# Top-1-group, top-2-expert MoE on one core: experts in fours with 32 places each, rows gathered and results added by one-hot products

## The chip, the cores and the metric

The kernel runs on one core of one Trainium2 chip. The metric is the device time of one execution in microseconds (us). Before the change three runs took 1572.35, 1572.91 and 1574.51 us, with a median of 1572.91 us.

## What is computed

The reference is a two-layer decoder trunk on 512 tokens of width 1024, in float32. Layer 0 mixes tokens with an S5 state space and an RG-LRU, layer 1 with multi-head latent attention. After each mixer comes a mixture of experts (MoE), and this is what the change touches. There are 64 experts in 8 groups of 8. Each token takes its best group and the best two experts in it:

```python
g_sel = jnp.argmax(g_logits, axis=-1)
top_vals, top_idx = lax.top_k(e_in_group, 2)
gates = p_g[:, None] * jax.nn.softmax(top_vals, axis=-1)
expert_id = g_sel[:, None] * 8 + top_idx
def expert_block(xb, e):                 # xb: the rows of the tokens that chose e
    return (silu(xb @ w1[e]) * (xb @ w3[e])) @ w2[e]   # 1024 -> 256 -> 1024
out = zeros.at[token].add(gate * expert_block(...))
```

So 1024 (token, expert) assignments fall on 64 experts, 16 on average, and every expert's three matrices (1 MiB each, 192 MiB for a layer) are read once. Counted from the reference on its own drawn inputs, the assignments of one expert are unequal: in layer 0 five experts have more than 32 (33, 33, 36, 40 and 61), in layer 1 four (33, 34, 37 and 39), and none has more than 64.

## The kernel before

The MoE of a layer is a sweep over 32 pairs of experts. An expert has 64 places (`CAP = 64`), so that a pair fills 128 rows: expert g of the pair sits in columns 64g to 64g+63 of the systolic array. Six experts' weights are in SBUF at a time: `w13[b]` holds w1 and w3 of slot b, `w2[b]` its w2. The slots lie in `ring`, `wbuf` and `region_a`, and belong to pairs in turn.

For a pair, TensorE does in this order: `te_up` (8 blocks of the 1024 inputs times 2 experts, 512 columns each, L1534), `te_xtrans` (8 transposes of the next pair's 128 rows, L1524), `te_hidden` (2 transposes, L1543) and `te_down` (8 products of 512 columns, L1554). A float32 product is carried out as two MATMUL instructions, so `te_up` is 32 of them and `te_down` 16; a transpose is one. ScalarE does the SiLU and half of the evacuations, VectorE the gating product (L1671) and the other half.

The rows come and go through DRAM. The normed rows are stored in `hrow`; GpSimd gathers each expert's rows with an indirect DMA into `xin` (L1478) and scatters its results with another into `ytok` (L1490), in quarters of 16 rows. When all is scattered, SyncE loads `ytok` back (`combine_sync`, L1902), and VectorE adds each token's two rows, weighted, to `x` (`gathered`, L558). The first pair's rows and the last pair's results go by one-hot products instead (L1280, L1593).

SyncE's queue carries the weight loads, in the order of the pairs: `up_weights_load` (L1744) waits until the slot's last user has done `te_up`, `down_weights_load` (L1749) until it has done `te_down`. The engines run the sweep in hardware loops (`Fori`).

Experts with more assignments than places get overflow blocks: `extra_blocks` runs once before the last pair, on two overflow blocks at a time, `OVPAIR` turns of a loop in which only the first `nov` do anything. With 64 places `nov` is 0 and the whole loop is jumped over.

Of the kernel before, what the change touches and what calls it, by code (L numbers as in the profile page):

```python
# [6 lines left out]
F32 = mybir.dt.float32  # L7
I32 = mybir.dt.int32
# [23 lines left out]
CAP = 64  # L32
QUART = CAP // 4
OVMAX = 2 * T // CAP - 1
NBLK = NE + OVMAX + 1
PAIR = 2 * CAP
NPAIR = NE // 2
# [7 lines left out]
NOROW = 8 * T  # L45
# [3 lines left out]
C_T, C_E, C_I, C_DESC, C_INVF = 576, 1088, 1152, 1168, 1176  # L49
C_ID8 = 1208  # L50
C_END = 1216


def shape_constants():

    c = np.zeros((P, C_END), np.float32)
    r = np.arange(P)
    c[:, C_ID:C_ID + P] = np.eye(P)
    c[:, C_UP:C_UP + P] = r[:, None] < r[None, :]
    c[:, C_ONE:C_ONE + P] = 1.0  # L60
# [8 lines left out]
    c[:, C_ID8:C_ID8 + 8] = r[:, None] + P * np.arange(8)[None, :] - NOROW  # L69
    return c  # L70


def hybrid_decoder(nc, a, out):
    ctx = ExitStack()
    with ctx:
# [25 lines left out]
        id2 = con[:, C_ID2:C_ID2 + CAP]  # L101
# [35 lines left out]
        s_zf = sem("s_zf")  # L137
# [19 lines left out]
        def alink(ins):  # L157
# [7 lines left out]
        junk = [r3[:, 0:1024], extra[:, 2048:3072], extra[:, 0:1024], extra[:, 2560:3584]]  # L165
# [306 lines left out]
        def even_scalar():  # L472
# [28 lines left out]
            S.wait_ge(s_zf, 128)  # L501
# [298 lines left out]
        win = [r2[:, n * KC * HW:(n + 1) * KC * HW].rearrange("p (k n) -> p k n", k=KC) for n in range(2)]  # L800
# [251 lines left out]
        def odd_vector():  # L1052
# [76 lines left out]
            for n in range(H * TC + 7):  # L1129
# [31 lines left out]
        R = extra[:, 2048:3072]  # L1161
        R2 = extra[:, 3072:4096]
# [8 lines left out]
        o2 = R[:, 928:960].rearrange("p (c g) -> p c g", c=TC)  # L1171
        ovb, ovs = R2[:, 64:128], R2[:, 128:192]
        quart, short, wrap, turn16 = R2[:, 0:64], R2[:, 64:128], R2[:, 128:192], R2[:, 448:512]
        place = R2[:, 192:448].rearrange("p (c e) -> p c e", c=TC)
        o12 = R[:, 896:960].rearrange("p (j c e) -> p j c e", j=2, c=TC)
        mm = R2[:, 512:768].rearrange("p (c e) -> p c e", c=TC)
        wk = R2[:, 768:1024].rearrange("p (c e) -> p c e", c=TC)
        gmx, v1, v2, pg, g12, tm = small(4), small(4), small(4), small(4), small(8), small(4)
        destf, blkf, base8, ov8, tm12 = small(8), small(8), small(8), small(8), small(8)
        tmg, gb, vd = small(4), small(4), small(4)  # L1180
        lastf = small(8)
        rk01 = R[:, 960:968].rearrange("p (c g) -> p c g", c=TC)
        ovf = small(17)
        ovw = R[0:1, :].rearrange("p (i e) -> p i e", i=16)
        w13 = [ring[b][:, 0:2, :] for b in range(RING)]
        w13 += [v.rearrange("p (a n) -> p a n", a=2) for v in (wbuf[:, 0:4096], rega[:, :])]
        w2 = [ring[b][:, 2, :] for b in range(RING)] + [wbuf[:, 4096:6144], wbuf[:, 6144:8192]]
        SLOTS = len(w2) // 2
        TURNS = [len(range(b, NPAIR, SLOTS)) for b in range(SLOTS)]


        xin = [regb[:, i * 1024:(i + 1) * 1024] for i in range(2)]
        xtr = [regb[:, 2048 + i * 1024:2048 + (i + 1) * 1024].rearrange("p (k s) -> p k s", k=KC) for i in range(2)]
        hid = [extra[:, i * DE:(i + 1) * DE] for i in range(2)]
        hidT = [extra[:, 512 + i * FC * PAIR:512 + (i + 1) * FC * PAIR].rearrange("p (f s) -> p f s", f=FC)
                for i in range(2)]
        yo = [extra[:, 1024 + i * D:1024 + (i + 1) * D] for i in range(2)]
        hot_s = extra[:, 0:8 * CAP].rearrange("p (j s) -> p j s", j=8)
        hot_b = extra[:, 512:512 + 8 * NE].rearrange("p (j b) -> p j b", j=8)
        oh0 = R[:, 160:672].rearrange("p (c s) -> p c s", c=TC)  # L1200
        hotv_s = R2[:, 192:704].rearrange("p (j s) -> p j s", j=8)
        hotv_b = R2[:, 704:832].rearrange("p (j b) -> p j b", j=8)
        gath = [v.rearrange("p (b d) -> p b d", b=4) for v in (rega[:, :], r0[:, 0:4096])]
        pickT = R2[:, 0:512].rearrange("p (c s) -> p c s", c=TC)
        pick = R2[:, 512:1024].rearrange("p (c s) -> p c s", c=TC)
# [7 lines left out]
        s_oh0 = sem("s_oh0")  # L1213
        s_fr, s_fre = sem("s_fr"), sem("s_fre")
        s_hot, s_hp = sem("s_hot"), sem("s_hp")
        s_dst = sem("s_dst")
        s_ov = sem("s_ov")
        s_hst = sem("s_hst")
        s_pk, s_pkt, s_pke = sem("s_pk"), sem("s_pkt"), sem("s_pke")
        s_fin = sem("s_fin")  # L1220

        ml = {n: [sem(f"{n}{l}") for l in range(2)] for n in (
            "s_xtp", "s_xte", "s_up", "s_si", "s_ac", "s_ht", "s_hte", "s_dn", "s_ye",
            "s_ga", "s_ow", "s_ox", "s_ostep", "s_oys")}
        s_xi = [[sem(f"s_xi{l}{j}") for j in range(2)] for l in range(2)]
        s_yst = [[sem(f"s_yst{l}{j}") for j in range(2)] for l in range(2)]
        s_w13 = [sem(f"s_w13{b}") for b in range(SLOTS)]
        s_w2 = [sem(f"s_w2{b}") for b in range(SLOTS)]  # L1230

# [40 lines left out]

        def first_rows_tensor(l):

            keep_clock(1)

            for c in range(TC):
                TE.wait_ge(s_oh0, TC * l + c + 1)
                for nh in range(2):
                    last = TE.matmul(ps[:, 2 + nh, :], oh0[:, c, :], h[:, c, nh * 512:(nh + 1) * 512],  # L1280
                                     start=c == 0, stop=c == TC - 1)
            last.then_inc(s_fr, 1)

        def first_trans_tensor(l):

            TE.wait_ge(s_fre, 2 * l + 2)
            for k in range(KC):
                last = TE.transpose(ps[:, k // 4, (k % 4) * PAIR:(k % 4 + 1) * PAIR], xin_block(0, k), ident)
            last.then_inc(ml["s_xtp"][l], 1)

        def table_tensor(l):

            for j in range(8):
                TE.wait_ge(s_hot, 9 * l + j + 1)
                last = TE.matmul(ps[0:CAP, 6, 0:NE], hot_s[:, j, :], hot_b[:, j, :], start=j == 0, stop=j == 7)
            last.then_inc(s_hp, 1)

        def extra_table_tensor(l):

            TE.wait_ge(s_hot, 9 * l + 9)  # L1300
            for j in range(8):
                last = TE.matmul(ps[0:CAP, 5, 0:NBLK - NE], hotv_s[:, j, :], hotv_b[:, j, :], start=j == 0, stop=j == 7)
            last.then_inc(s_hp, 1)

        def first_max(oneh, val, best, order):
# [4 lines left out]
            vlink(V.reduce_max(order, t8, AX.X))  # L1310
            tt(oneh, t8, order[:, :, None].to_broadcast([P, TC, 8]), ALU.is_equal)
# [9 lines left out]
        def turned_ranks(rk):  # L1321

            ts(short, quart, CAP / QUART - 1.5, ALU.is_lt)
            stt(turn16.rearrange("p (a e) -> p a e", e=16), quart.rearrange("p (a e) -> p a e", e=16), 1.0,
                con[:, C_I:C_I + 16][:, None, :].to_broadcast([P, NE // 16, 16]), ALU.add, ALU.mult)
            tt(turn16, turn16, short, ALU.mult)
            vlink(V.memset(turn16[:, 0:2], 0.0))
            ts(wrap, quart, float(QUART), ALU.mult, float(QUART + 8 * T), ALU.add)
            stt(wrap, short, -8.0 * T, wrap, ALU.mult, ALU.add)
            wrapb = wrap[:, None, :].to_broadcast([P, TC, NE])  # L1330
            tt(place, rk, turn16[:, None, :].to_broadcast([P, TC, NE]), ALU.add)
            tt(wk, place, wrapb, ALU.is_ge)
            tt(wk, wk, wrapb, ALU.mult)
            tt(place, place, wk, ALU.subtract)

        def route_vector(l):
# [3 lines left out]
            first_max(oh, gl, gmx, tmg)  # L1340
# [31 lines left out]
            for j in range(2, CAP // QUART):  # L1372
                stt(quart, cnt, float(QUART * j), quart, ALU.is_gt, ALU.add)
# [759 lines left out]
```

## Time and profile before

| | |
|---|---|
| median of three runs | 1572.91 us |
| span of the profiled execution, first to last instruction | 1571.5 us |
| TensorE busy | 1344.6 us, 86% of the span |
| VectorE, ScalarE, GpSimd busy | 491.8, 295.4 and 290.5 us |
| MoE sweep of layer 0 on TensorE, first `te_up` to last `te_down` | 246.9 to 747.5 us |
| MoE sweep of layer 1 | 1051.0 to 1554.9 us |

The profiled execution's own time is its span of 1571.5 us, 1.4 us below the median of the runs. PE is TensorE's matmul side and PEld its loads of the stationary operand. Busy shares are averages over stages with different limits, so stages are read one by one.

### The profile page before, as it was taken

What the parts mean: (1) busy time and instruction counts of PE and PEld (TensorE: products, weight loads), DVE (VectorE), ACT (ScalarE), POOL (GpSimd) and SP (SyncE); (2) the same over time, 40 slices, a digit from 0 to 9 for tenths busy, and PEclk for the clock granted to TensorE, in tenths of its full rate; (3) what the DMA queues carried; (4) which work ended last, traced back from release to release, by engine and by line L of the source; (5) the groups of instructions that cost most, each with busy time, mean ns of one, the idle gap of its engine ahead of it and who ended that gap; (6) DMA issues with size and microseconds to landing.
All of it is one profiled execution on the core that took longest, in us unless ns stands there. A gap on an engine that the chain in (4) does not pass through costs nothing.

```text
span 1571.5 us, 19548 instructions
## 1 busy us (share of the span) xinstructions
PE 1344.6 (86%) x6176; PEld 624.6 (40%) x6176; DVE 491.8 (31%) x1034; ACT 295.4 (19%) x584; POOL 290.5 (18%) x412
## 2 busy tenths in 40 slices
PE   7999998987887878878799899999978878878786
PEld 5555463332332323333464565453323323333332
DVE  7996145211111111112605572253111111111114
ACT  6236111110010010101235642111100100101000
POOL 2104002332222222222000000003322222222220
PEclk9999999999899998999799899999999998999999
DMA  5423845999999999999410307049999999999996
GB/s 211 166 103 131 347 176 220 374 393 405 405 397 404 403 396 412 397 401 380 174 54 1 121 1 294 23 172 389 402 394 404 390 392 403 404 411 404 394 397 276
DMA packets 83427, 472.17 MB, mean 300 GB/s; under 512 B 13953, under 2 KB 16145, under 8 KB 32816
## 3 DMA queue, kind: packets, MB, share of 16 engines
q1 hardware_dynamic: 69792, 445.25, 71.7%
q0 software_dynamic: 11568, 19.90, 3.8%
q10 hardware_dynamic: 2016, 6.34, 1.0%
q8 instruction: 33, 0.54, 0.1%
q14 instruction: 18, 0.15, 0.0%
HBM read 453.54 MB, written 27.39 MB: 306 GB/s over the span
## 4 chain that ended last, share of the span: by engine, by line
PE 42%; SPq 35%; DVE 11%; DMA 6%; issue 5%; ACT 1%; DVEq 0%; POOL 0%; ACTq 0%; POOLq 0%
SPq L1744 23%; PE ps L1534 13%; SPq L1749 12%; PE ps L1554 5%; DMA ring<-in_moe_w 4%; PE ps L442 4%; PE ps L885 3%; PE ps L904 2%; PE ps L315 2%; PE ps L908 2%; PE ps L431 2%; PE ps L391 2%; PE ps L1524 1%; DVE extra L549 1%; DVE x L558 1%
## 5 line engine op out<-in xcount | busy, mean ns | idle before, releaser
L1534 PE MATMUL ps<-ring,region_b 128*64 128x512 f32 x1408 | 348.8, 653 | 78.2 <-issue 51.3
L1534 PEld LDWEIGHTS ps<-ring,region_b 128*64 128x64 f32 x1408 | 118.2, 150 | 305.8 <-issue 267.1
L1671 DVE TENSOR_TENSOR extra<-extra,ps 128x256 f32<-128x256 f32 x64 | 26.9, 421 | 579.8 <-ACT extra L1608 544.9
L1534 PE MATMUL ps<-wbuf,region_b 128*64 128x512 f32 x320 | 159.6, 657 | 40.0 <-DMA region_a<-in_moe_w 22.2
L1554 PE MATMUL ps<-ring,extra 128*64 128x512 f32 x704 | 160.8, 598 | 34.0 <-DVE extra L1677 31.7
L1534 PE MATMUL ps<-region_a,region_b 128*64 128x512 f32 x320 | 159.8, 658 | 0.0
L1478 POOL DMA_INDIRECT region_b<-hrow,icol x120 | 111.4, 928 | 147.9 <-issue 147.9
L1608 ACT ACTIVATE extra<-ps 128x256 f32<-128x256 f32 x64 | 24.5, 383 | 585.3 <-PE ps L1534 551.7
L1490 POOL DMA_INDIRECT ytok<-extra,icol x120 | 106.1, 884 | 152.6 <-issue 152.6
L1684 DVE COPY extra<-ps 128x512 f32<-128x512 f32 x64 | 44.3, 692 | 241.7 <-PE ps L1554 241.6
L1534 PEld LDWEIGHTS ps<-wbuf,region_b 128*64 128x64 f32 x320 | 46.6, 150 | 145.7 <-issue 136.9
L1554 PEld LDWEIGHTS ps<-ring,extra 128*64 128x64 f32 x704 | 49.9, 136 | 114.5 <-issue 91.5
L1614 ACT ACTIVATE extra<-ps 128x512 f32<-128x512 f32 x64 | 38.2, 597 | 276.2 <-PE ps L1554 276.2
L1554 PE MATMUL ps<-wbuf,extra 128*64 128x512 f32 x320 | 73.1, 597 | 16.7 <-DVE extra L1677 15.7
L1488 POOL COPY icol<-blkidx 64x2 int32 x60 | 12.4, 206 | 399.5 <-DVE extra L1684 399.5
L1524 PEld LDWEIGHTS ps<-con,region_b 128*128 128x128 f32 x496 | 60.0, 194 | 50.3 <-issue 50.3
L1524 PE MATMUL ps<-con,region_b 128*128 128x128 f32 x496 | 71.8, 288 | 0.0
L315 PE MATMUL ps<-region_b,wbuf 128*128 128x512 f32 x128 | 55.8, 594 | 0.0
L1601 ACT ACTIVATE region_b<-ps 128x512 f32<-128x512 f32 x64 | 38.2, 597 | 50.5 <-PE ps L1524 32.6
L1666 DVE COPY region_b<-ps 128x512 f32<-128x512 f32 x62 | 42.9, 692 | 12.9 <-PE ps L1524 9.8
L1534 PEld LDWEIGHTS ps<-region_a,region_b 128*64 128x64 f32 x320 | 46.6, 150 | 0.0
L1554 PEld LDWEIGHTS ps<-wbuf,extra 128*64 128x64 f32 x320 | 23.6, 136 | 52.3 <-issue 44.8
(322 smaller groups left out, 1511.8 us busy)
## 6 DMA issues: line engine op xcount, KB each, us to landing
ring<-in_moe_w SPq DMA_DIRECT2D x264, 1024.0 KB
wbuf<-in_moe_w SPq DMA_DIRECT2D x80, 1024.0 KB
region_a<-in_moe_w SPq DMA_DIRECT2D x40, 1024.0 KB
ytok<-ring SPq DMA_DIRECT2D x8, 1024.0 KB, 10.2
wbuf<-in_ev_w_in SPq DMA_DIRECT2D x3, 2048.0 KB, 14.3
wbuf<-in_ev_w_out SPq DMA_DIRECT2D x2, 2048.0 KB, 14.6
hrow<-region_a ACTq DMA_DIRECT2D x8, 512.0 KB, 10.4
region_a<-ytok SPq DMA_DIRECT2D x8, 512.0 KB, 5.0
```

The lines of the kernel that those rows point to most:

```text
L315: last = TE.matmul(ps[:, bank, :], w[:, k, m * P:(m + 1) * P], hT[:, k, :], start=k == 0, stop=k == KC - 1)
L442: last = TE.matmul(ps[:, 4 + (n + 2) % 4, :], lhs(k, n // 2), wout[n % 2][:, k, :], start=k == 0, stop=k == KC - 1)
L885: last = TE.matmul(ps[:, 4 * n + c, 0:HW], hT[:, k, c * P:(c + 1) * P], win[n][:, k, :], start=k == 0, stop=k == KC - 1)
L1478: G.indirect_dma_start(xin[j][CAP * g:CAP * g + n, :], None, hrow[l], bass.IndirectOffsetOnAxis(ap=icol[0:n, 2 * j + g:2 * j + g + 1], axi ...
L1490: G.indirect_dma_start(ytok[l], bass.IndirectOffsetOnAxis(ap=icol[0:n, 4 + 2 * j + g:5 + 2 * j + g], axis=0), yo[j][CAP * g:CAP * g + n, : ...
L1524: last = TE.transpose(ps[:, k // 4, (k % 4) * PAIR:(k % 4 + 1) * PAIR], xin_block(j, k), ident)
L1534: last = TE.matmul(ps[CAP * g:CAP * (g + 1), 2 + j, :], xtr[j][:, k, CAP * g:CAP * (g + 1)], up_weights(2 * slot + g, k), start=k == 0, st ...
L1554: last = TE.matmul(ps[CAP * g:CAP * (g + 1), 6 + nh, :], hidT[j][:, f, CAP * g:CAP * (g + 1)], w2[2 * slot + g][:, f * D + nh * 512:f * D ...
L1666: V.tensor_copy(xtr[j][:, 0:4, :].rearrange("p k s -> p (k s)"), ps[:, 0, :])\
L1684: V.tensor_copy(yo[j][:, 0:512], ps[:, 6, :]).then_inc(ml["s_ye"][l], 1)
L1744: nc.sync.dma_start(w13[b][:, n, :], src).then_inc(s, 16)
L1749: nc.sync.dma_start(w2[b], src).then_inc(s, 16)
```

## The change

- An expert has 32 places instead of 64 (`CAP = 32`). Experts go in fours (`NQ = 16` fours a layer), each in a 32-column strip of the array. There are still six slots of weights, now dealt to single experts; the slot in `region_a` moves to `extra`, because the normed rows `h` in `region_a` are now read throughout the sweep. New scratch space `scr` takes the routing's tables.
- `te_rows` gathers the four experts' rows, already transposed, as products of h (stationary) with a one-hot matrix (moving). `te_back` transposes the one-hot matrix weighted by the gates, and `te_combine` multiplies it with the results; VectorE adds the eight 512-column halves to `x` (`added`). `hrow`, `ytok`, the zero fill of `ytok`, all indirect DMAs, the index tables and GpSimd's part of the sweep are gone.
- The sweep is written out in full for all 16 fours and both layers; only the overflow keeps a loop. It works on two blocks of 32 places, before the last four, with loads, one-hot products, and additions to `x` of its own. `OVPAIR` is 16. With the counts above there are 5 overflow blocks in layer 0 and 4 in layer 1, so `nov` is 3 and 2.
- The loads of the attention's `mla_w_uq` and of one half of `mla_w_in` wait for the last four but one (and stand behind the overflow in SyncE's queue); the other half waits for the last `te_up`.

```diff
-CAP = 64
+CAP = 32
+ROWS = 4 * CAP
+NQ = NE // 4
+        def h_block(c, k):
+            return h[:, c, :].rearrange("p (q k) -> p k q", k=KC)[:, k, :]
+        def te_rows(n):
+            TE.wait_ge(s_hot, n + 1)
+            if n:
+                TE.wait_ge(s_xte, 2 * n)
+            for k in range(KC):
+                for c in range(TC):
+                    last = TE.matmul(ps[:, k // 4, (k % 4) * ROWS:(k % 4 + 1) * ROWS], h_block(c, k), hotc[:, c, :],
+                                     start=k % 4 == 0 and c == 0, stop=k % 4 == 3 and c == TC - 1)
+        def te_combine(n):
+            for i in range(8):
+                    TE.wait_ge(s_ca, 8 * n + max(i - 2, 0))
+                TE.matmul(ps[:, SUMS[i % 3], :], back[n % 2][:, i // 2, :], yo[:, (i % 2) * 512:(i % 2 + 1) * 512],
+                          start=True, stop=True).then_inc(s_cb, 1)
         def moe_tensor(l):
-            with TE.Fori(0, 4) as i:
-                for n in range(2, 8):
-                    one(6 * i + n, n, 2 * i + n // SLOTS)
+            te_rows(NQ * l)
+            te_back(NQ * l)
+            for q in range(NQ):
+                n = NQ * l + q
+                te_up(n)
+                if q:
+                    te_combine(n - 1)
+                te_hidden(n)
+                if q < NQ - 1:
+                    te_back(n + 1)
+                    te_rows(n + 1)
+                te_down(n)
+                if q == NQ - 2:
+                    extra_tensor(l, overflow(TE, l))
+            te_combine(NQ * l + NQ - 1)
         def moe_sync(l):
+            for q in range(1, NQ):
+                for e in range(4 * q, 4 * q + 4):
+                    if e >= SLOTS:
+                        SP.wait_ge(s_up, NQ * l + (e - SLOTS) // 4 + 1)
+                        up_load(l, e)
+                for e in range(4 * q, 4 * q + 4):
+                    if e >= SLOTS:
+                        SP.wait_ge(s_dn, 2 * (NQ * l + (e - SLOTS) // 4) + 2)
+                        down_load(l, e)
         def extra_sync(l):
                         for g in range(2):
                             e = SP.value_load(ovi[0:1, bass.ds(2 * i + g, 1)], min_val=0, max_val=NE - 1)
-                            up_weights_load(g, l, e, ml["s_ow"][l])
+                            up_weights_load(4 + g, l, e, s_ow[l])
-                        SP.wait_ge(ml["s_oys"][l], 32 * (i + 1))
+                        SP.wait_ge(s_ostep[l], STEPS * (i + 1))
```

TensorE's program, one pair of the sweep before, in the part ahead of the loop. A row is the line of the call, the operation, what it writes and reads (moving operand first, then stationary), its shape and what it waits for.

```order
L1534 MATMUL ps<-ring,region_b 64x512 [waits s_w130,s_xte0]
L1534 MATMUL ps<-ring,region_b 64x512 x15
L1524 MATMUL ps<-con,region_b 128x128 [waits s_xi01,s_xte0]
L1524 MATMUL ps<-con,region_b 128x128 x7
L1543 MATMUL ps<-con,extra 128x128 [waits s_ac0]
L1543 MATMUL ps<-con,extra 128x128
L1554 MATMUL ps<-ring,extra 64x512 [waits s_w20,s_hte0]
L1554 MATMUL ps<-ring,extra 64x512 x7
```

The same place after the change, one four in the middle of the sweep.

```order
L1425 MATMUL ps<-ring,region_b 32x512 [waits s_w132,s_w133,s_w131,s_ac,s_w130,s_xte]
L1425 MATMUL ps<-ring,region_b 32x512 x31
L1461 MATMUL ps<-region_b 128x512 [waits s_ca,s_bke,s_ye]
L1461 MATMUL ps<-region_b 128x512 [waits s_ca] x7
L1434 MATMUL ps<-con,scr 128x128 [waits s_hte,s_ac]
L1434 MATMUL ps<-con,scr 128x128
L1411 MATMUL ps<-con,region_b 128x128 [waits s_bke,s_hotg]
L1411 MATMUL ps<-con,region_b 128x128 x3
L1400 MATMUL ps<-region_b,region_a 128x128 [waits s_xte,s_hot]
L1400 MATMUL ps<-region_b,region_a 128x128 x31
L1450 MATMUL ps<-ring,scr 32x512 [waits s_w22,s_w23,s_w21,s_ca,s_w20,s_hte]
L1450 MATMUL ps<-ring,scr 32x512 x15
```

Two pairs become one four: the up and down products are as many as for two pairs, now in strips of 32 columns. The combining products (L1461), the transposes of the gate matrix (L1411) and 32 gathering products (L1400) are new; the 8 transposes of rows (L1524) are gone.

SyncE's queue after the change at the overflow, which before was jumped over: the body of the loop, and what follows it.

```order
L1735 UNCONDITIONAL_BRANCH [waits s_dn]
L1736 COMPARE_AND_BRANCH
...
L1587 DMA wbuf<-in_moe_w 128x2048 x2
L1592 DMA wbuf<-in_moe_w 128x2048
...
L1587 DMA extra<-in_moe_w 128x2048 x2
L1592 DMA wbuf<-in_moe_w 128x2048
...
L1736 UNCONDITIONAL_BRANCH [waits s_ostep0]
L1735 REGISTER_ALU
L1735 COMPARE_AND_BRANCH
L1733 UNCONDITIONAL_BRANCH
L1781 DMA wbuf<-in_mla_w_uq 128x3x1536 [waits s_dn]
```

Each turn loads two experts again (6 MiB) and holds the queue until VectorE's last addition of that turn (s_ostep0); the attention's weights come behind the loop.

## Rows read from the trace of the kernel before

**Rows 1.** The page: what DMA moved in 40 slices of the span.

```profile
GB/s 211 166 103 131 347 176 220 374 393 405 405 397 404 403 396 412 397 401 380 174 54 1 121 1 294 23 172 389 402 394 404 390 392 403 404 411 404 394 397 276
```

**Rows 2.** The two sweeps as windows of the span.

```profile
core 0: us, PE busy (x) PEld busy (x) DVE busy (x) ACT busy (x) POOL busy (x), PEclk, DMA share, GB/s
300.00:730.00 430.00, 350.07 (x1566) 137.01 (x1562) 59.82 (x118) 42.00 (x80) 105.34 (x159) 0.94 1.02 400
1060.00:1540.00 480.00, 397.83 (x1790) 156.99 (x1786) 75.70 (x157) 49.39 (x94) 120.13 (x180) 0.94 1.01 399
```

**Rows 3.** DMA queues: packets, MB, share of 16 engines' time over the span.

```profile
q1 hardware_dynamic: 69792, 445.25, 71.7%
q0 software_dynamic: 11568, 19.90, 3.8%
```

**Rows 4.** The chain that ended last, in order of time: start us, us, what.

```profile
246.87 8.78 PE ps L1534 x32
...
261.51 6.87 PE ps L1534 x32
...
274.23 6.87 PE ps L1534 x32
```

**Rows 5.** Groups by line and shape: busy us, mean ns of one, idle before.

```profile
L399 PE MATMUL ps<-ring 128*32 128x128 f32 x128 | 3.7, 273 | 0.0
L399 PEld LDWEIGHTS ps<-ring 128*32 128x32 f32 x128 | 3.4, 110 | 0.8 <-issue 0.8
L1251 PEld LDWEIGHTS ps<-rwb,region_b 128*128 128x128 f32 x128 | 14.8, 192 | 0.2
L310 PEld LDWEIGHTS ps<-wbuf,region_b 128*128 128x128 f32 x64 | 19.6, 309 | 8.6 <-ACT region_b L188 1.1
L347 PE MATMUL ps<-ring 128*128 128x128 f32 x64 | 7.4, 277 | 1.1 <-ACT ring L497 1.1
```

**Rows 6.** VectorE and ScalarE groups by line and shape, same columns.

```profile
L549 DVE TENSOR_TENSOR extra<-extra 128x256 f32<-128x256 f32 x12 | 5.1, 425 | 0.4
L1918 DVE TENSOR_TENSOR x<-ps,x 128x512 f32<-128x512 f32 x16 | 10.3, 685 | 0.2
L717 DVE TENSOR_TENSOR extra<-ps,ring 128x1024 f32<-128x1024 f32 x2 | 2.4, 1222 | 0.1
L1608 ACT ACTIVATE extra<-ps 128x256 f32<-128x256 f32 x64 | 24.5, 383 | 585.3 <-PE ps L1534 551.7
```

**Rows 7.** Timeline around the first and the last products of layer 0's sweep.

```profile
231.02 0.70 PE L1264 MATMUL ps<-extra,con 128*128 128x256 f32 x2 [1.15 <-DVEq L1351]
...
731.40 3.65 PE L1554 MATMUL ps<-ring,extra 128*64 128x512 f32 x16 [0.52 <-DVE extra L1677]
734.89 7.04 PE L1534 MATMUL ps<-ring,region_b 128*64 128x512 f32 x32
...
743.89 3.65 PE L1554 MATMUL ps<-ring,extra 128*64 128x512 f32 x16 [0.52 <-DVE extra L1677]
...
752.78 8.49 PE L1593 MATMUL ps<-extra 128*128 128x512 f32 x16 [5.24 <-DVE extra L1684]
...
767.22 1.28 DVE L1918 TENSOR_TENSOR x<-ps,x 128x512 f32<-128x512 f32 x2
...
774.74 21.51 PE L885 MATMUL ps<-ring,region_b 128*128 128x352 f32 x64 [0.83 <-ACT region_b L188]
```

**Rows 8.** The chain in layer 1: first `te_up`, last `te_down`.

```profile
1051.04 9.50 PE ps L1534 x32
...
1551.17 3.68 PE ps L1554 x16
```

**Rows 9.** The chain inside SyncE's loop end (L1773).

```profile
585.51 0.03 SPq L1773
...
585.63 0.20 issue
```

**Rows 10.** The page: DMA issues, KB each, us to landing.

```profile
out<-x ACTq DMA_DIRECT2D x4, 512.0 KB, 2.6
```

More of the change, by code:

```diff
@@ L1197, in hybrid_decoder @@
[L1197 to L1203, printed above, removed]
@@ L1271, in route_tensor, with first_max @@
             last.then_inc(s_rc, 1)
-        def first_rows_tensor(l):
             keep_clock(1)
[L1277 to L1305, printed above, removed]
+        def first_max(oneh, val, best):
             vlink(V.reduce_max(best, val, AX.X))
@@ L1527, in te_up @@
-        def te_up(l, p, j, slot, turn, first):
-            TE.wait_ge(ml["s_xte"][l], 2 * p + 2)
-            TE.wait_ge(s_w13[slot], 64 * (TURNS[slot] * l + turn + 1))
-            if not first:
-                TE.wait_ge(ml["s_ac"][l], p - 1)
-            for k in range(KC):
-                for g in range(2):
-                    last = TE.matmul(ps[CAP * g:CAP * (g + 1), 2 + j, :], xtr[j][:, k, CAP * g:CAP * (g + 1)],
-                                     up_weights(2 * slot + g, k), start=k == 0, stop=k == KC - 1)
-            last.then_inc(ml["s_up"][l], 1)
@@ new lines, in te_back, with te_up @@
+        def te_back(n):
+            TE.wait_ge(s_hotg, n + 1)
+            if n:
+                TE.wait_ge(s_bke, n)
+            for c in range(TC):
+                last = TE.transpose(ps[:, 4, c * P:(c + 1) * P], hotgc[:, c, :], ident)
+            last.then_inc(s_bk, 1)
+        def te_up(n):
+            l, q = n // NQ, n % NQ
+            TE.wait_ge(s_xte, 2 * n + 2)
+            for g in range(4):
+                e = 4 * q + g
+                TE.wait_ge(s_w13[e % SLOTS], 32 * turn(l, e))
+            if n:
+                TE.wait_ge(s_ac, n)
+            for k in range(KC):
+                for g in range(4):
+                    r = slice(CAP * g, CAP * (g + 1))
+                    last = TE.matmul(ps[r, 2, :], xtr[:, k, r], up_weights((4 * q + g) % SLOTS, k),
+                                     start=k == 0, stop=k == KC - 1)
+            last.then_inc(s_up, 1)
@@ new lines, in te_hidden, with te_down @@
+        def te_hidden(n):
+            TE.wait_ge(s_ac, n + 1)
+            if n:
+                TE.wait_ge(s_hte, n)
+            for f in range(FC):
+                last = TE.transpose(ps[:, 5, f * ROWS:(f + 1) * ROWS], hid_block(hid, f), ident)
+            last.then_inc(s_ht, 1)
+        def te_down(n):
+            l, q = n // NQ, n % NQ
+            TE.wait_ge(s_hte, n + 1)
+            for g in range(4):
+                e = 4 * q + g
+                TE.wait_ge(s_w2[e % SLOTS], 16 * turn(l, e))
+            if n:
+                TE.wait_ge(s_ca, 8 * n)
```

827 lines of the change are left out of this document (320 added, 507 removed).

## The prediction, made before the changed kernel was run

> **What bounds the kernel now.** I read the two sweeps first, as stages. The slices [rows 1] show some 400 GB/s from slice 9 to 19 and from 28 to 39 and much less elsewhere; over both sweeps as windows the DMA engines are full (share 1.02 and 1.01), at 400 and 399 GB/s, while PE is busy 81% and 83% of the time [rows 2]. So memory bounds them. The chain [rows 4] shows what TensorE could do where weights are there: `te_up` to `te_up` of the next pair is 12.7 us (261.51 to 274.23). A pair's weights are 6.29 MB, 15.7 us at 400 GB/s. The reader is to see that TensorE has 19% to spare, and that anything that only helps TensorE is worth nothing there.
>
> What else the DMA engines carry: the software queue (GpSimd's gathers and scatters, mostly) has 19.90 MB and 3.8% of the engines' time [rows 3], 60 us of the span. Without it the weights could come up to that much earlier. That is the gain on offer, some 25 us a layer, if nothing else becomes the bound.
>
> **TensorE per four, step by step.** A 512-column MATMUL on 64 array columns runs two at a time: 32 of them in 6.87 us [rows 4], a slot of 0.43 us. *Strips:* with 32 columns, do four run at a time? L399 is a product of 32-column strips now: 128 instructions of 128 columns in 3.7 us, 29 ns each [rows 5], where one full-width instruction of 128 columns takes 116 ns (L347, 64 in 7.4 us). So four at a time. A four then costs 64 × 0.43 / 4 = 6.9 us up and 32 × 0.43 / 4 = 3.4 us down, half of two pairs.
>
> *Combining:* 8 products of full width, 16 instructions at 0.43: 6.9 us. VectorE's additions (8 × 0.69 us [rows 6]) keep pace behind three banks. *Transposes:* six at 0.12, 0.8 us. *Gathering:* 32 products, 64 MATMULs of 128 columns, each with its own load of 128 columns. No product like it exists: its stationary operand, `h_block`, is read with a stride of 8 words. The nearest row is L310, float32 products whose stationary operand has a stride of 4: its load records last 309 ns, those of contiguous L1251 192 ns [rows 5]. A record is longer than the slot that it takes: L1251's 128 loads lie in 14.8 us, 116 ns each, and L399's in 3.4 us, 27 ns, with a record of 110. The excess is 76 to 83 ns, so a strided load should take about 309 − 80 = 229 ns, twice a contiguous one. At L310 512 columns hide it; here 128 (116 ns) don't. I take 64 × 0.229 = 14.7 us; bounds 64 × 0.116 = 7.4 (no cost of the stride) and 64 × 0.309 = 19.8.
>
> The Trainium skill (TensorE: Matmul & The Clock Gate, LDWEIGHTS) gives a load's time as its columns over 1.2 ns, 107 ns for 128, and names no stride. L1251 agrees, L310 speaks against it; by the rule the gather would be 6.8 us and the time that of the second case below.
>
> Sum of a four: 6.9 + 6.9 + 0.8 + 14.7 + 3.4, and 0.5 for the seams: 33.2 us. Two pairs' weights, 12.58 MB, need 31.2 us at 403 GB/s. So the bound passes from DMA to TensorE, just, and the 60 us of the software queue are not collected. SyncE's queue doesn't starve it: the last two `te_up` weights of a four are issued when the previous four's `te_up` ends, and 26 us of TensorE's work follow, against 21 for what stands in the queue.
>
> **The sweep.** *Start:* ranks are done at 231.7 [rows 7]; place 0.5, one-hot 0.8, gather 14.7, copies 0.8: first `te_up` at 248.5 where it is 246.9 now: +1.6 us a layer. *Middle:* first four 6.9 + 1.0 (SiLU, gating) + 0.8 + 14.7 + 3.4 = 26.8; 14 × 33.2 = 464.8; last one without gather 17.8: 509.4 us. Now: 246.87 to 747.54, 500.7 [rows 4, 7], and 1051.04 to 1554.85, 503.8 [rows 8]: +8.7 and +5.6. *End:* in layer 0 it is 27.2 us from the last `te_down` to L885, with the wait for scattered rows in it [rows 7]. After: copies 0.8, first product 0.9, eight additions 5.5, two row steps of the norm about 3.2, and the 6.2 that follow the last addition now (768.5 to 774.7): 16.6, so −10.6. In layer 1 it is 16.7 to the end of the span; after: 0.8, eight products and an addition 7.6, store 2.6 [rows 10] and 0.5: 11.5, −5.2. Both layers: +1.6 + 8.7 − 10.6 + 1.6 + 5.6 − 5.2 = +1.7 us. Leaving out the zero fill, `hrow` and GpSimd's tables I cost at nothing: they are off the chain. Without overflow the change would be a wash, 1573 us.
>
> **The overflow.** With 32 places nine experts spill. The drawn inputs give 5 blocks in layer 0 (33, 33, 36, 40 and 61 assignments) and 4 in layer 1, hence 3 + 2 = 5 turns that have never run before. In a turn everything waits in a row. SyncE loads 6.29 MB, 15.7 us at 400 GB/s, and 1.3 to start (the 2.6 of a 512 KB store less its bytes [rows 10]); at the same time VectorE makes the one-hots (six passes of 0.43 [rows 6], seams: 3.2), TensorE gathers (64 MATMULs, by loads again 14.7, transposes 0.5), VectorE copies 1.6: 20.0 us. Then up 6.9, SiLU and gating 1.0, transposes and copy 0.7, down 3.65, copy 1.3 (L717), and four times two products (1.7) and a 1024-wide addition (1.2) with their handshakes: 12.6. That is 26.1. And after idle time TensorE comes back slower: 8.78 us for what takes 6.87 [rows 4], 8.49 for L1593's sixteen [rows 7]; I add 3. A turn: 49 us; the first of a layer 51, its loads standing behind the last four's. SyncE can't issue the next turn's loads before the last addition, so nothing overlaps. Layer 0: 51 + 49 + 49 = 149; layer 1: 100. The other 27 turns of `OVPAIR` (13 and 14) are empty: at 0.3 us, what SyncE's loop end takes [rows 9], 8 us. At most 3.5 each: now `te_up` follows a jump over the same loop without a gap, behind 3.65 us of `te_down` [rows 7]. Together 257 us.
>
> Sum against the profiled execution: 1571.5 + 1.7 + 257 = 1830. It lies 1.4 below the median of the runs: **1832 us**.
>
> **The rivals.**
> - *The stride costs nothing.* Gather 7.4, a four 25.9: DMA stays the bound and the software queue's time comes back. After the first `te_up` 182.5 MB remain, 453 us at 403 GB/s, and 4 us until the first `te_down` frees slots; the sweep from first `te_up` to last `te_down` is 6.9 + 4 + 453 + 3.4 = 467.3, it starts 5.7 earlier; −97 for both layers with the ends. The overflow costs 271, its loads being queued behind more. 1571.5 − 97 + 271 + 1.4 = 1747. For it: L1251's slot; against it: L310's record.
> - *The gather is dearer,* 0.309 a load: 5.1 more for 32 gathers and in five turns: 1832 + 185 = 2017.
> - *Empty turns are dear.* TensorE's loop body is some 300 instructions, jumped over 27 times. At 3.5 us a turn: 1832 + 86 = 1918. The Trainium skill (Runtime: NRT & Kernel Launch, Instruction fetch mechanics) says a taken branch to a target outside the two pages at hand stalls for a fetch; no row here shows such a stall, and the rule also favours a written-out sweep.
> - *Strips run two at a time* with 512 columns: 10.3 more a four, 2160 us. L399 speaks against it.
> - *Not slower.* If no expert spills on the chip, the turns fall away: 1575, or 1476 without the stride's cost. In place of that the turns would have to be cheap: with the 97 us of the first rival they decide at 19 us each, and the loads alone take 15.7 before any of 26 us of dependent work.
>
> **How the numbers follow.** Chances: as summed 0.48, stride free 0.22, dear empty turns 0.12, dearer gather 0.08, two at a time 0.03, no spill 0.04, something else 0.03. The range takes in the first three: 1745 to 1930. A measurement of this kernel tells 0.2% from no change: faster 0.02, same 0.02, slower 0.96.
>
> **What the profile would show.** Right: GB/s in the sweeps down to some 380 with DMA share about 0.95, PE above 95% and its granted clock near 1.0; 64 gathering MATMULs in 14.7 us; two stretches of 149 and 100 us with PE half idle, five bursts of 6 MiB in them. Wrong: GB/s at 403 with waits for weights in every four (stride free); `te_up` of a four at 13.7 us (strips); a pause of tens of us behind the last turn (empty turns). The forecast fails most easily in the turns' count and price: 5 × 10% is 25 us.

## The result and the profile after

The changed kernel takes 1899.79 us (median of four runs, 1899.06 to 1902.1), the kernel before 1572.63 beside it: a ratio of 1.2075, 95% interval 1.2056 to 1.2095. The profiled execution has a span of 1897.9 us, 326.4 more than before.

The page of the changed kernel, in 40 slices of the span: TensorE's granted clock in tenths and what DMA moved. The lines below them are the DMA queues (packets, MB, share of 16 engines).

```profile
PEclk9999999999999999666699999999999999998667
GB/s 175 45 24 365 160 127 392 368 383 389 359 392 358 391 386 365 79 133 133 111 1 45 100 1 288 111 161 391 358 393 380 370 387 362 391 358 391 62 115 45
q1 hardware_dynamic: 70656, 459.91, 59.3%
q0 software_dynamic: 1312, 3.63, 0.6%
```

Against [rows 1] the sweeps fell from some 400 to some 380 GB/s. Behind each stands a slow stretch, at 79 to 133 GB/s in layer 0 and at 62 to 115 in layer 1, where the granted clock falls to 0.6. Of the software queue's 19.90 MB [rows 3] 3.63 are left, but the sweeps didn't get faster by it. Windows of one sweep, of the first two overflow turns of layer 0, of the second turn's gather, of the first turn's combining and of the pause behind layer 1's:

```profile
core 0: us, PE busy (x) PEld busy (x) DVE busy (x) ACT busy (x) POOL busy (x), PEclk, DMA share, GB/s
278.70:747.00 468.30, 467.75 (x2552) 308.40 (x2544) 135.71 (x220) 30.92 (x57) 0.00 (x0) 1.00 0.91 377
745.60:804.60 59.00, 43.08 (x142) 23.55 (x134) 10.55 (x17) 0.97 (x2) 0.00 (x0) 0.66 0.35 143
804.60:860.60 56.00, 42.54 (x134) 23.64 (x134) 11.04 (x19) 0.38 (x1) 0.00 (x0) 0.62 0.27 112
808.80:816.00 7.20, 7.20 (x32) 7.20 (x32) 0.00 (x0) 0.00 (x0) 0.00 (x0) 0.50 1.01 427
788.00:804.00 16.00, 11.44 (x13) 3.49 (x12) 3.97 (x4) 0.00 (x0) 0.00 (x0) 0.50 0.00 0
1853.60:1864.80 11.20, 0.00 (x0) 0.03 (x1) 0.01 (x1) 0.00 (x0) 0.00 (x0) 0.50 0.00 0
```

In the sweep TensorE now works 467.75 of 468.3 us and DMA has 9% to spare: the bound has passed to it, where [rows 2] had DMA full and TensorE idle for 19%. The chain (start us, us, what) shows a four, from one `te_up` (L1425) to the next:

```profile
1605.31 6.87 PE ps L1425 x64
1612.18 7.06 PE ps L1461 x16
1619.24 0.23 PE ps L1434 x2
1619.47 0.44 PE ps L1411 x4
1619.91 15.24 PE ps L1400 x64
1635.14 3.57 PE ps L1450 x32
1638.71 6.87 PE ps L1425 x64
```

33.4 us, and the gather (L1400) is nearly half. `te_up` has 64 instructions in the time that a pair's 32 took [rows 4]: four strips run at once. In the groups, a gather's load record is 335 ns (L310 had 309, L1251 192 [rows 5]), and its slot 15.24 / 64 = 0.238 us:

```profile
L1400 PEld LDWEIGHTS ps<-region_b,region_a 128*128 128x128 f32 x2048 | 490.2, 335 | 0.7 <-DVE region_b L1336 0.5
```

The chain through the second turn and the end of the third:

```profile
809.00 15.12 PE ps L1643 x64
...
825.91 8.58 PE ps L1653 x32
...
836.37 3.64 PE ps L1668 x16
...
845.36 3.76 PE ps L1675 x4
849.14 1.24 DVE x L1720
...
898.28 1.97 PE ps L1675 x4
...
911.96 3.76 PE ps L1675 x4
915.74 1.24 DVE x L1720
916.98 10.45 issue
927.43 2.74 PE ps L1425 x9
```

Everything in a turn waits in a row, as foretold; the products L1675 take 3.76 us where the third turn's first takes 1.97 (4 instructions each), at a granted clock of 0.50, the lower of the two levels (1.2 of 2.4 GHz). The 10.45 us of "issue" stand where the loop runs through its thirteen empty turns.

The ledger by stage, before to after, in us (the sweeps without their overflow; the last column is what the prediction had):

| stage | before | after | change | foretold |
|---|---|---|---|---|
| start to first `te_up`, layer 0 | 246.9 | 251.1 | +4.2 | +1.6 |
| sweep, layer 0 | 500.7 | 516.3 | +15.6 | +8.7 |
| end of layer 0 to L885 (now L874) | 27.2 | 16.9 | −10.3 | −10.6 |
| L885 to layer 1's first `te_up` | 276.3 | 278.3 | +2.0 | +1.6 |
| sweep, layer 1 | 503.8 | 517.0 | +13.2 | +5.6 |
| end of layer 1 | 16.7 | 11.6 | −5.1 | −5.2 |
| overflow, both layers | 0 | 306.7 | +306.7 | +257 |

### The profile page after: what moved, and what is told of

It reads as the page before. It is cut to its first block, busy times and chain, and to the rows that moved or that the text cites. A ratio compares the mean times of both kernels' runs of the same rounds, so it can differ in the third digit from the quotient of the medians.

```text
span 1897.9 us, 21547 instructions
## 1 busy us (share of the span) xinstructions
PE 1758.7 (93%) x8822; PEld 1102.8 (58%) x8822; DVE 644.0 (34%) x1163; ACT 263.4 (14%) x521; POOL 41.5 (2%) x43
## 3 DMA queue, kind: packets, MB, share of 16 engines
q0 software_dynamic: 1312, 3.63, 0.6%
## 4 chain that ended last, share of the span: by engine, by line
PE 85%; DVE 8%; DMA 3%; issue 3%; ACT 1%; SPq 1%; DVEq 0%; ACTq 0%
PE ps L1400 26%; PE ps L1425 12%; PE ps L1461 12%; PE ps L1450 6%; PE ps L1675 4%; PE ps L431 3%; PE ps L1653 2%; PE ps L1643 2%; PE ps L874 2%; DMA wbuf<-in_moe_w 2%; PE ps L893 2%; PE ps L304 1%; PE ps L897 1%; PE ps L420 1%; PE ps L380 1%
## 5 line engine op out<-in xcount | busy, mean ns | idle before, releaser
L1400 PE MATMUL ps<-region_b,region_a 128*128 128x128 f32 x2048 | 492.5, 401 | 0.0
L1400 PEld LDWEIGHTS ps<-region_b,region_a 128*128 128x128 f32 x2048 | 490.2, 335 | 0.7 <-DVE region_b L1336 0.5
L1425 PE MATMUL ps<-ring,region_b 128*32 128x512 f32 x1408 | 229.9, 606 | 24.7 <-issue 24.2
L1461 PE MATMUL ps<-region_b 128*128 128x512 f32 x512 | 228.5, 599 | 2.8 <-ACT region_b L1504 1.4
L1522 DVE TENSOR_TENSOR x<-ps,x 128x512 f32<-128x512 f32 x256 | 176.7, 691 | 48.0 <-PE ps L1461 44.9
L1461 PEld LDWEIGHTS ps<-region_b 128*128 128x128 f32 x512 | 94.5, 190 | 137.3 <-issue 131.8
L1425 PEld LDWEIGHTS ps<-ring,region_b 128*32 128x32 f32 x1408 | 63.1, 112 | 134.5 <-issue 133.6
L1425 PE MATMUL ps<-extra,region_b 128*32 128x512 f32 x320 | 140.6, 592 | 0.0
L1425 PE MATMUL ps<-wbuf,region_b 128*32 128x512 f32 x320 | 140.6, 592 | 0.0
L1450 PE MATMUL ps<-ring,scr 128*32 128x512 f32 x704 | 116.2, 595 | 1.8 <-DVE scr L1539 1.8
L1675 PE MATMUL ps<-region_b,scr 64*128 64x512 f32 x80 | 67.0, 983 | 28.1 <-DVE x L1720 21.1
L1450 PE MATMUL ps<-wbuf,scr 128*32 128x512 f32 x320 | 72.5, 595 | 0.0
L1425 PEld LDWEIGHTS ps<-wbuf,region_b 128*32 128x32 f32 x320 | 35.2, 110 | 47.9 <-issue 47.9
L1675 PEld LDWEIGHTS ps<-region_b,scr 64*128 64x128 f32 x80 | 20.8, 287 | 71.0 <-issue 71.0
L1653 PE MATMUL ps<-wbuf,scr 128*32 128x512 f32 x80 | 45.4, 733 | 16.2 <-DMA wbuf<-in_moe_w 10.8
L304 PE MATMUL ps<-region_b,wbuf 128*128 128x512 f32 x128 | 55.8, 594 | 0.0
```

Of the source, the lines that this page charges most:

```text
L304: last = TE.matmul(ps[:, bank, :], w[:, k, m * P:(m + 1) * P], hT[:, k, :], start=k == 0, stop=k == KC - 1)
L1400: last = TE.matmul(ps[:, k // 4, (k % 4) * ROWS:(k % 4 + 1) * ROWS], h_block(c, k), hotc[:, c, :], start=k % 4 == 0 and c == 0, stop=k % 4 ...
L1425: last = TE.matmul(ps[r, 2, :], xtr[:, k, r], up_weights((4 * q + g) % SLOTS, k), start=k == 0, stop=k == KC - 1)
L1450: last = TE.matmul(ps[r, 6 + nh, :], hidT[:, f, r], w2[(4 * q + g) % SLOTS][:, at:at + 512], start=f == 0, stop=f == FC - 1)
L1461: TE.matmul(ps[:, SUMS[i % 3], :], back[n % 2][:, i // 2, :], yo[:, (i % 2) * 512:(i % 2 + 1) * 512], start=True, stop=True).then_inc(s_cb, 1)
L1522: V.tensor_tensor(xs, ps[:, SUMS[i % 3], :], xs, ALU.add).then_inc(s_ca, 1)
```

## Experiments

Each is compared with the kernel before in runs beside it; two kernels leave out part of the computation, and their expectations say which.

**Where the time goes: the stride, the overflow, the empty turns, the banks.** Four changes of the changed kernel, one at a time. *e1* stores h so that a block's 128 columns lie side by side:

```diff
-            V.scalar_tensor_tensor(h[:, c, :], x[:, c, :], rstd[:, c:c + 1], gain[:, :],
+            V.scalar_tensor_tensor(h[:, c, :].rearrange("p (k q) -> p q k", k=KC),
+                                   x[:, c, :].rearrange("p (q k) -> p q k", k=KC), rstd[:, c:c + 1],
+                                   gain[:, :].rearrange("p (q k) -> p q k", k=KC),
...
-            return h[:, c, :].rearrange("p (q k) -> p k q", k=KC)[:, k, :]
+            return h[:, c, k * P:(k + 1) * P]
```

> The changed kernel with h stored so that a stationary block of 128 columns lies in one piece (VectorE writes it with a stride instead); everything else is the same. Theory (a strided stationary load takes twice the slot): the 64 gathering MATMULs of a four go from 15.3 us to 7.4 to 8.0 us, TensorE's work of a four from 33.4 to some 26 us, the sweeps become DMA-bound at 31.2 us a four, 395 to 405 GB/s: about 92 us less in all, 1795 to 1825 us, with waits for weights before te_up. Rival (the gather is slow for another reason: its accumulation into quarters of a bank, or its one-hot moving operand): 15.3 us as before, and 1898 us.

1774.95 us, ratio 1.1277 (1.1244 to 1.131): 125 us less than the change and below the expected 1795 to 1825. A gather of 64 takes 7.16 us, so the theory holds. The sweep is bound by memory again, and at 421 GB/s, not at 400, which the range had not allowed for (window, columns as above):

```profile
278.00:700.00 422.00, 375.40 (x2544) 211.11 (x2542) 131.84 (x209) 30.07 (x55) 0.00 (x0) 0.94 1.01 421
```

The groups:

```profile
L1402 PEld LDWEIGHTS ps<-region_b,region_a 128*128 128x128 f32 x2048 | 231.4, 192 | 1.0 <-DVE region_b L1338 0.5 <-issue 0.4
L186 DVE SCALAR_TENSOR_TENSOR region_a<-x,smalls,gain 128x1024 f32<-128x1024 f32 x16 | 32.1, 2005 | 0.6
```

The load's record is back at L1251's 192 ns. The price is a strided write by VectorE: 2005 ns a norm row, 1285 before. In the windows of the two sweeps (300:730 before, 278:700 here) the hardware queues moved 164.8 MB in 430 us before, 383 GB/s, and 177.2 MB in 422 us here, 420. The software queue moved 7.2 MB in that window before, 17 GB/s, with 5% of the engines' time; it moved nothing here. So the weights gained 37 GB/s, more than what the software queue itself had moved. That its transfers slowed the others is likely, but not shown: the order of the loads changed too, and no run takes out the queue alone. The rival "stride free" (1747) was right that with a load at its contiguous price DMA stays the bound; it was wrong about this layout, about the 403 GB/s, and about the overflow (271 us for the 306 of e5 below).

*e2* sets the number of turns to zero:

```diff
-            ts(ovf[0:1, 32:33], ovs[0:1, NE - 1:NE], 0.5, ALU.mult, 0.25, ALU.add)
+            ts(ovf[0:1, 32:33], ovs[0:1, NE - 1:NE], 0.0, ALU.mult, 0.25, ALU.add)
```

> The changed kernel with the number of overflow turns set to 0; it leaves out the results of the assignments beyond 32 places. Theory (the overflow costs what its place in the trace shows, 180.9 + 125.8 us, and everything that it delays is merely shifted): 1583 to 1598 us, within 1.5% of the kernel before. Rival (part of it overlaps work that then has to be done elsewhere): above 1620 us.

1591.79 us, ratio 1.0113 (1.0084 to 1.0143). As expected (1583 to 1598), the overflow costs 308 us, all but some 18 us of the whole loss.

*e3* cuts the loop to the turns that are needed, `OVPAIR = 3`:

> The changed kernel with the overflow loop of 3 turns instead of 16, which is enough for these inputs. Theory (an empty turn costs TensorE 0.80 us, and there are 27 of them now, 1 then): the pause behind the last real turn shrinks from 10.5 and 11.2 us to 0.5 to 1.5 us, 1874 to 1880 us. Rival (the pause is paid once for leaving the loop, a fetch of code, whatever the number of turns): the pauses stay, 1895 to 1900 us.

1881.92 us, ratio 1.1957 (1.1922 to 1.1992), 2 us above the expected 1874 to 1880. The chain behind layer 0's third turn, and behind layer 1's second, where one empty turn is left:

```profile
917.21 0.74 issue
917.95 7.41 PE ps L1425 x37
```

```profile
1846.18 1.51 issue
```

The pause is 0.74 us without an empty turn, 1.51 with one, 10.45 with thirteen and 11.18 with fourteen. So it is 0.74 us for leaving and 0.75 for each empty turn, not 0.80: the 27 empty turns take 20 us, and with the leaving the two pauses 21.6. Of the 19 that 26 empty turns make, 18 come back in the time. The rival, a pause paid once whatever the number of turns, is out.

*e4* writes a turn's 16 combining instructions to eight PSUM banks, one behind another, where they shared two (the wait moves ahead of the loop over c):

```diff
-                    TE.wait_ge(st, STEPS * i + OYE + 2 * c)
...
-                        last = TE.matmul(ps[:, 6 + nh, :], xback[:, c, :], xyo[:, nh * 512:(nh + 1) * 512],
...
+                        last = TE.matmul(ps[:, (6, 0, 2, 4)[c] + nh, :], xback[:, c, :],
```

> The changed kernel with the eight combining products of an overflow turn in eight PSUM banks, back to back, instead of in two banks with a wait for VectorE's addition after each pair. Theory A (the waits keep the clock at half and cost themselves): from first product to last addition 17.6 us become 8.5 to 10 us, five times, 1855 to 1863 us. Theory B (the clock has fallen before, in the wait for the copy, and stays low through the eight products): 16 MATMULs at 0.94 us, 15 us and an addition, 1888 to 1893 us.

1867.49 us, ratio 1.1865 (1.1809 to 1.1921), with 7 us between its two runs. That lies between its two theories (1855 to 1863 and 1888 to 1893), and neither held. In the three turns of layer 0, and windows of the first two of these rows:

```profile
786.06 11.61 PE L1676 MATMUL ps<-region_b,scr 64*128 64x512 f32 x16 [1.40 <-DVE region_b L1718]
835.23 7.10 PE L1676 MATMUL ps<-region_b,scr 64*128 64x512 f32 x16 [1.40 <-DVE region_b L1718]
881.45 11.43 PE L1676 MATMUL ps<-region_b,scr 64*128 64x512 f32 x16 [1.40 <-DVE region_b L1718]
```

```profile
786.10:797.60 11.50, 11.50 (x16) 4.17 (x16) 3.67 (x3) 0.00 (x0) 0.00 (x0) 0.60 0.00 0
835.20:842.30 7.10, 7.07 (x16) 2.91 (x16) 3.67 (x3) 0.00 (x0) 0.00 (x0) 1.00 0.00 0
```

The same 16 instructions take 7.10 us at a granted 1.00 and 11.5 at 0.60, with nothing to wait for between them. So a turn's end is dear in part by its handshakes, which are gone here, and in part by the clock, which differs from turn to turn.

**The ceiling.** *e5* is e1 and e2 together.

> The block order of e1 and no overflow turns, together: it leaves out the assignments beyond 32 of an expert. Theory: with the gather at a contiguous load's slot the sweeps are bound by memory at the 421 GB/s that e1 showed, and the overflow costs what it cost beside e1, 27 us for the first turn of a layer and its rest: 1465 to 1490 us, the only form of the change that beats the kernel before (1573). Rival, that the overflow costs less beside a sweep bound by memory, because its loads are the next ones in the queue anyway: 1500 to 1520.

1468.85 us, ratio 0.9328 (0.9309 to 0.9347), within 1465 to 1490. That is what fours and one-hot products are worth without overflow: 105 us against the kernel before beside it (1574.0). In e1 the overflow costs 1774.95 − 1468.85 = 306 us, as much as beside a sweep bound by TensorE (308), so the rival of a cheaper overflow is out.

**The clock.** *e7* fills the turn's pauses with products that nobody reads, three ahead of the wait for the one-hots, one ahead of those for the copies, the gating and each addition:

```diff
+            def keep(n):
+                for _ in range(n):
+                    TE.matmul(ps[:, 3, :], ident, h[:, 0, 0:512], start=True, stop=True)
...
+                keep(3)
                 TE.wait_ge(st, STEPS * i + OG)
...
+                    keep(1)
                     TE.wait_ge(st, STEPS * i + OYE + 2 * c)
```

> The changed kernel with filler products in the overflow's pauses alone: three 512-column products of the identity into a bank that nobody reads ahead of the wait for the one-hots, one ahead of the waits for the copies, the gating and each addition. Nothing else moves. Theory, the granted clock: the turns lose about 8 us each to the 1.2 GHz level (5.3 in the products of the combining, 2 in te_up's start, 0.5 in the transposes; nothing in the strided gather, which takes 15.1 us at 0.50 as at 1.00), so with the clock held at 2.4 GHz the time falls by 30 to 40 us, to 1860 to 1870, and the later products of a turn take 1.97 us where they took 3.75. Rival, the handshakes: the pauses themselves are the cost, the fillers only stand in the way of what comes next, 1900 to 1915.

1873.21 us, ratio 1.1901 (1.1875 to 1.1926): 27 us less than the change (ratios 1.2075 and 1.1901), with more work, and 3 us above the expected 1860 to 1870. The windows of its first two turns, and from the chain the products of the first:

```profile
747.00:801.00 54.00, 47.42 (x153) 25.59 (x154) 10.71 (x18) 0.38 (x1) 0.00 (x0) 0.81 0.38 156
801.00:854.00 53.00, 49.08 (x157) 26.32 (x156) 12.36 (x22) 0.38 (x1) 0.00 (x0) 0.84 0.33 132
```

```profile
789.94 1.97 PE ps L1683 x4
791.93 1.24 DVE x L1728
...
793.30 1.97 PE ps L1683 x4
```

All four product steps take 1.97 us, in every turn. So the handshakes alone don't make them slow; the low clock does. The gain is 13 us short of the 40 at best: `te_up` still takes 9.66 us for 6.87 behind a layer's first wait for weights, and some 8 in the later turns, and some fillers stand in the chain themselves (1.06 us ahead of the transposes, 1.81 behind the gather).

**All parts together.** *e6* is e1, e3 and e4, with the next turn's weights asked for at the end of `te_down`; *e8* adds e7's fillers.

> Block order of e1, 3 turns in the loop, the turn's products in eight banks, and the next turn's weights asked for when te_down of this turn has ended rather than after its last addition. From e1's 1775: -18 for the 27 empty turns, -25 to -30 for the products (three rounds of copy, signal and 3.75 us fewer in each of five turns), 0 to -5 for the earlier load, since the gather of a turn at the 1.2 GHz level ends no sooner than the load: 1720 to 1735 us. Rival, that the turns wait for their weights: the earlier load then takes 3 us more off each of three turns, 1705 to 1715.

> e6 with the fillers of e7. With a contiguous load the clock decides the gather too: a load of 128 columns takes 0.112 us at 2.4 GHz and 0.212 at 1.2. If the clock holds, a turn is 3 (one-hots) + 0.5 + 7.2 + 1.8 + 6.9 + 1.6 + 3.6 + 1.4 + 6.9 + 1.2 = 34 us, the first of a layer 27 + 22 = 49 because of its load; with e5's 1475 that is 1475 + 2 x 49 + 3 x 34 = 1675, range 1660 to 1700. Rival, that the fillers themselves run at 1.2 GHz and delay the turn: no gain over e6, 1720 to 1735.

e6: 1726.26 us, ratio 1.0972 (1.0946 to 1.0999). e8: 1681.26 us, ratio 1.0678 (1.066 to 1.0696). Both lie where their theories put them, and what differs between them is the fillers, worth 45 us here. Layer 0's second and third turn in e8 are 38.3 and 35.3 us, where 34 had been put. Below are 64 gathering products of contiguous h in the overflow with a window in that stretch, first of e6 (granted clock 0.50), then of e8 (1.00):

```profile
735.26 13.75 PE L1646 MATMUL ps<-scr,region_a 128*128 128x64 f32 x64
735.30:749.00 13.70, 13.70 (x65) 13.53 (x64) 0.00 (x0) 0.00 (x0) 0.00 (x0) 0.50 0.29 124
```

```profile
740.67 7.26 PE L1651 MATMUL ps<-scr,region_a 128*128 128x64 f32 x64
741.00:747.00 6.00, 6.00 (x57) 6.00 (x55) 0.00 (x0) 0.00 (x0) 0.00 (x0) 1.00 0.15 60
```

**The overflow as fours.** What is left of a turn in e8 is a row of dependent steps on 64 rows. *e9* rebuilds the overflow: up to four blocks in a turn, in the sweep's own tiles, between the last four's `te_down` and its combining; two turns written out; weights queued behind the last four's, in slots 4, 5, 0, 1 and then 2, 3, 0, 1; one-hots made during the last `te_up`; single fillers in the pauses. It has room for 8 overflow blocks a layer, where the change has it for 32. `np` is the number of pairs of blocks, 3 and 2:

```diff
-                if q == NQ - 2:
-                    extra_tensor(l, overflow(TE, l))
+            extra_tensor(l, overflow(TE, l))
             te_combine(NQ * l + NQ - 1)
...
+            with TE.If(0 < np):
+                body(0)
+            with TE.If(2 < np):
+                body(1)
```

> The block order of e1, and the overflow rebuilt as further fours: up to four blocks in a turn, in the sweep's own tiles, behind te_down of the last four and ahead of its combining; the turns are written out twice (room for 8 blocks, the inputs have 5 and 4), VectorE makes the one-hots while te_up of the last four runs, and the weights queue behind the last four's without a pause. Layer 0 has two turns (4 blocks and 1), layer 1 one. Theory: what is left of the overflow is its weights. From te_up of the last four, DMA still has its down weights (10 us), then w1 and w3 of four experts (21), then their w2 (10): te_down of the turn starts at about 42 us, and copy, products, last addition and the four's own combining end 20 us later; without a turn the sweep ends at 26. So about 36 us in layer 1, and 16 more in layer 0 for the pair of the second turn: 88 us on e5's 1469 gives 1557, range 1545 to 1580, at or a little below the kernel before. Rival, that the branches, the register loads of SyncE and the low clock after each wait for weights cost as much again as in the small turns: 1590 to 1620.

1574.33 us, ratio 1.0013 (1.0002 to 1.0024): the time of the kernel before, 325 us below the change. That is 17 us above the 1557 of its sum. In layer 0 the turns take 32.7 us each and wait for no weights. The second had been put at 16 us, the time of its pair's weights alone, and that is the 17 us. In layer 1 the wait for the pair's last weights does end last ahead of `te_down`, by 1.2 us, and 4.05 us of "issue" stand behind the turn; the rival's figure (1590 to 1620) is far off all the same.

*e10* mends what its chain shows: norm rows in order where no gather reads them, a copy released by its own transposes, and a wait at a turn's end for the last addition but one:

```diff
+            if n in (0, 2):
+                V.scalar_tensor_tensor(h[:, c, :], x[:, c, :], rstd[:, c:c + 1], gain[:, :],
...
+                last.then_inc(s_xb[l], 1)
+                if j:
+                    wt(o, 16 * j)
...
-                wt(o, 16 * j + 16)
+                wt(o, 16 * j + 15)
```

> e9 with three small repairs of what its chain shows in the turns. The strided norm row (2.01 us, against 1.285) is kept only for the two norms ahead of the experts, where the gather reads it: some six row steps off the chain, 3 to 4 us. The copy of the gated one-hots is released by its own transposes and no longer stands ahead of te_up's (0.5 and a signal of 0.2, three turns: 2 us). A turn no longer waits for its last addition before the next product, whose bank that addition doesn't touch (1.5 us, three times: 4.5). Together 9 us: 1562 to 1568 us, ratio 0.995 to 0.998. Rival, that these steps lie beside DMA waits: under 3 us, ratio 1.000 to 1.002 as e9.

1562.33 us, ratio 0.9933 (0.992 to 0.9946): 10 us below the kernel before, and the fastest version that leaves nothing out for these inputs.

Its chain through layer 0's first turn, and the start of the second:

```profile
702.79 0.63 PE ps L1646 x4
703.42 7.15 PE ps L1652 x64
...
712.03 7.07 PE ps L1664 x64
...
721.84 3.64 PE ps L1682 x32
...
726.53 6.96 PE ps L1690 x16
...
733.52 1.24 DVE x L1761
...
734.89 7.38 PE ps L1652 x64
```

A turn of up to four experts takes 32 us, where the change spent 56 on two. One step of the expectation failed: the next turn still waits for the last addition, by the wait for 16 ahead of its gather, so only the transposes moved up.

*e11* reads x with a stride of 8 words and writes h in order:

> e10 with the norm row of the experts' norms written in order and read with a stride of 8 words, in place of read in order and written with a stride of 128. If VectorE pays for the strided write alone, a row falls from 2.0 us to 1.3, 4 us less than e10 in all: 1558 to 1564. If it pays for any stride, as for the write, the time is that of e10.

1563.84 us, ratio 0.9945 (0.993 to 0.9959), that of e10. A row takes 2.09 us read with a stride, 2.00 written with one: VectorE pays for either.

## Why the prediction was right

It said 1832 us, 1745 to 1930, slower; it is 1899.8. The likeliest case was the one that came, and one term of its sum, the overflow, was mis-sized.

- *Four strips at a time:* right, 6.87 us for 64 instructions. *Combining* 7.06 (6.9), *down* 3.57 (3.4).
- *The gather:* right. 0.238 us a load against 0.229 from L310's record less the excess; 15.24 us against 14.7. e1 shows that it is the layout of h: 7.16 us with its columns side by side. By the figure of the Trainium skill (TensorE: Matmul & The Clock Gate, LDWEIGHTS) 64 loads would take 6.8 us as an estimate. e1's contiguous loads agree; for the strided ones the trace disagrees with it and decides. One nearer row had been passed over: the transposes of the norms load this very h with the same stride, and 24 of them take 2.69 us before the change (L210), 0.112 a load. Taken for the gather they would have given the cheap case. So L310, a float32 product, was the right row to go by, and why a product pays for the stride and a transpose doesn't stays open.
- *A four* 33.4 us (33.2), and with it the passing of the bound from DMA to TensorE: right, PE 467.75 of 468.3 us. The 31.2 us for a four's weights rested on 403 GB/s as ceiling; at e1's 421 it is 29.9. That error cost nothing only because TensorE was the bound. Of the 6.9 us that the sweep of layer 0 is longer than foretold, 2.8 are in fourteen fours, 1.0 in the first (27.8), and 3.1 in the last (20.9 for 17.8): its `te_up` comes back from the pause at the low clock, 9.01 us for 6.87.
- *The start* was 2.6 us later than foretold: ahead of the first gather TensorE does the counts' products (0.89) and one that keeps the clock (0.91), 1.8 us that I had left out.
- *The ends:* right, −10.3 and −5.1.
- **The overflow was the mis-sized term:** 257 us foretold, 306.7 measured; that is 50 of the 68 us by which the time was missed. It falls apart into two. *A turn* was put at 49 us and the first at 51, 249 in all; they took 58.4, 55.8 and 56.4 in layer 0 and 58.8 and 55.8 in layer 1, 285 in all. Up to `te_up` the second turn took 21.1 us (20.0). From there on it took 34.7, where the sum had 26.1 and an allowance of 3 for TensorE's slow return from a pause. Most of that is the combining: from the first product to the next turn 19.2 us, 12.6 in the sum. I had taken the allowance from single bursts behind a pause [rows 4, 7], 1.9 and 1.6 us. But the clock doesn't fall once a turn and come back: it is at 1.00 from late in `te_up` to about the first product of the combining, and at 0.50 through the rest of the combining (window 788:804), the one-hots, the gather and the start of the next `te_up`. Three of four product steps nearly doubled by it, some 6 of the 6.6 us. e7 shows it by holding the clock. *Empty turns* were put at 0.3 us, with 3.5 as bound; they took 0.75 and 0.74 for leaving the loop (e3), 21.6 us where the sum had 8. The Trainium skill (Runtime: NRT & Kernel Launch, Instruction fetch mechanics) has a fetch stall where a branch leaves the pages at hand; the runs show the 0.75 us, and not what part of it is fetching.
- *The count of turns,* 3 and 2: right. *The signs:* 377 GB/s and a DMA share of 0.91 in the sweep, for 380 and 0.95. In the turns PE was 73 and 76% busy (43.08 of 59 us, 42.54 of 56), not half idle, since it worked at the low clock for long.
- *Rivals.* "Not slower" failed on its own condition: turns would have had to cost 19 us. Its number for no overflow was 1575, e2 gives 1592; for no overflow and no stride 1476, e5 gives 1469. "Stride free" had 1747 with overflow, e1 gives 1775.

What I had not weighed is that the overflow's cost belongs to its form and not to the 32 places: nine blocks cost 306 us as small serial turns, 212 (e8 less e5) with the clock held, the banks spread and the empty turns gone, and 105 (e9 less e5) as further fours.

## What to carry to other kernels

When a capacity is cut so that a path runs which never ran before, cost that path step by step, price TensorE in it at half its clock if its steps are short and each waits for another engine, and look first whether the spilled work can take the main loop's own form. A gathering product with few moving columns (128 here) is bound by its stationary load if that is strided: lay the columns of the stationary operand side by side, and pay for the stride on an engine that is off the path. A hardware loop with a large bound and few real turns is not free: its empty turns were 0.75 us each here.

## What the runs showed of the hardware

- In the gathering products a 128-column float32 load whose columns lie 8 words apart takes 0.24 us at either clock: 15.24 us for 64 at 1.00, 15.12 in a turn at a granted 0.50. A contiguous one takes twice as long at the low level: 7.16 to 7.26 us for 64 at 1.00, 13.75 at 0.50. So at the low level the stride costs little, and only at the high level twice the time.
- The same strided h as stationary operand of a transpose costs no such time. Eight loads of a norm row in the changed kernel, at a granted 1.00, are 0.12 us each:

```profile
961.22 0.97 PEld L199 LDWEIGHTS ps<-con,region_a 128*128 128x128 f32 x8 [1.62 <-DVE region_a L186]
```

  All 128 transposes were busy 18.9 us there and 19.5 in e9 with a contiguous h, though the median record of a load fell from 193 to 140 ns.
- With hardware queues alone e1's sweep moved 421 GB/s; with the indirect transfers beside them the two sweeps before moved 399 and 400 in all, 383 of it by the hardware queues in layer 0's. I had taken 403 for the ceiling.
- VectorE's 1024-wide norm row takes 1.285 us in order, 2.00 with a strided write, 2.09 with strided reads.
